# Mixer groups: the second gate block ahead of the turns of B and x, the rest one block later

## The reference

```
z, xbc, dt = split(u @ w_in)               # z: gate, xbc: x, B, C
xs, B, C = silu(causal_conv(xbc))
per chunk:  seg = exp(segment sums of dt*A)          # decay inside a chunk
            y   = (C B^T * seg) @ (x*dt) + exp(acs) * (C @ state)
            state = state * decay + B^T @ (x*dt * to_end)
y = rmsnorm((y + D*xs) * silu(z)) @ w_out
```

## Time and profile before

| | |
|---|---|
| median of 3 runs | 1906.42 us (1904.54 to 1907.23) |
| the profiled execution | 1900.23 us, span 1898.4 us |
| PE busy | 1832.8 us (97%) |
| weight loads of PE busy | 1742.0 us (92%) |
| DVE / ACT / POOL busy | 1140.4 / 825.7 / 249.8 us |
| mean granted clock of TensorE | 0.99 |
| the mixer's four groups | from 298 us to about 592 us of the span |

### The profile page before, as it was taken

How to read it: one execution, slowest core, us unless ns; L and a number is a source line. 1 busy time by engine, 2 the same in 40 slices (tenths; PEclk the granted TensorE clock), 3 DMA queues, 4 the chain that set the end, 5 groups by cost and what they waited for, 6 DMA issues and landing times.

```text
span 1898.4 us, 28238 instructions
## 1 busy us (share of the span) xinstructions
PE 1832.8 (97%) x10552; PEld 1742.0 (92%) x10552; DVE 1140.4 (60%) x1703; ACT 825.7 (43%) x1425; POOL 249.8 (13%) x298
## 2 busy tenths in 40 slices
PE   9999999999999999999999999988998999999997
PEld 8999998798887899999999999985777889999997
DVE  6554447878888655444765544455777746455444
ACT  5333325665464433333553333345665534333233
POOL 1000110422221000011400001222112130000110
PEclk9999999999999999999999999999999999999999
DMA  6444444456352544444344444441124533444441
GB/s 204 128 119 129 134 143 145 151 189 227 117 200 84 176 127 120 129 145 133 112 142 122 121 132 142 136 140 37 45 82 128 170 118 113 133 125 121 142 136 64
DMA packets 67652, 249.71 MB, mean 132 GB/s; under 512 B 8328, under 2 KB 9608, under 8 KB 66288
## 3 DMA queue, kind: packets, MB, share of 16 engines
q1 hardware_dynamic: 57584, 205.32, 35.9%
q0 software_dynamic: 9984, 43.24, 6.8%
HBM read 235.74 MB, written 12.12 MB: 131 GB/s over the span
## 4 chain that ended last, share of the span: by engine, by line
PE 83%; DVE 9%; ACT 4%; issue 2%; DMA 1%; POOL 0%; SPq 0%; DVEq 0%; ACTq 0%; POOLq 0%
PE pair L1805 23%; PE pair L1806 23%; PE pair L1807 23%; PE pair L2300 1%; PE pair L2218 1%; DVE wlo L1195 1%; PE pair L2219 1%; PE pair L2220 1%; DVE cy L1321 1%; PE pair L1812 1%; PE pair L1814 1%; PE pair L1813 1%; ACT seg L835 1%; PE pair L2002 1%; DVE S L1417 1%
## 5 line engine op out<-in xcount | busy, mean ns | idle before, releaser
L1805 PE MATMUL pair<-xh,whi 128*128 128x384 f32 x1928 | 652.9, 339 | 16.2 <-DVE xl L1205 13.4
L1806 PE MATMUL pair<-xl,whi 128*128 128x384 f32 x1928 | 647.1, 336 | 0.0
L1807 PE MATMUL pair<-xh,wlo 128*128 128x384 f32 x1928 | 646.9, 336 | 0.0
L1195 DVE TENSOR_TENSOR wlo<-raw,whi 128x1024 fp32r<-128x1024 f32 (+3 forms) x372 | 464.7, 1251 | 185.4 <-ACT whi L706 176.1
L706 ACT ACTIVATE whi<-raw 128x1024 fp32r<-128x1024 f32 (+2 forms) x369 | 378.7, 1029 | 290.8 <-PE pair L1807 276.7
L1805 PEld LDWEIGHTS pair<-xh,whi 128*128 128x128 f32 x1928 | 364.1, 189 | 26.3 <-issue 14.9
L1806 PEld LDWEIGHTS pair<-xl,whi 128*128 128x128 f32 x1928 | 364.3, 189 | 1.6 <-issue 1.0
L1807 PEld LDWEIGHTS pair<-xh,wlo 128*128 128x128 f32 x1928 | 364.1, 189 | 0.0
L1215 DVE TENSOR_TENSOR tg<-pair,rstd 128x384 f32<-128x384 f32 x88 | 49.0, 557 | 331.2 <-PE pair L1807 330.5
L1805 PE MATMUL pair<-ah,whi 128*128 128x384 f32 x704 | 237.0, 337 | 3.5 <-DVE tu L1216 3.3
L1807 PE MATMUL pair<-ah,wlo 128*128 128x384 f32 x704 | 236.6, 336 | 0.0
(11 more groups left out here) (394 smaller groups left out, 2285.1 us busy)
## 6 DMA issues: line engine op xcount, KB each, us to landing
raw<-in_stream SPq DMA_DIRECT2D x372, 512.0 KB, 3.6
S<-in_ssm POOLq DMA_DIRECT2D x4, 2048.0 KB, 9.2
out_ssm_s<-S POOLq DMA_DIRECT2D x4, 2048.0 KB, 8.1
seg<-acs_rows POOLq DMA_DIRECT2D x12, 512.0 KB, 6.1
cTb<-in_cacheT POOLq DMA_DIRECT2D x10, 512.0 KB, 4.0
kn<-rs_rows SPq DMA_DIRECT2D x16, 264.0 KB
lowC<-in_cache SPq DMA_DIRECT2D x8, 512.0 KB, 3.2
lowA<-in_cacheT POOLq DMA_DIRECT2D x6, 512.0 KB, 5.2
```

Of the source, the lines that this page charges most:

```text
L1195: V.tensor_tensor(wlo[:, r, 0:w], raw[:, r, 0:w], whi[:, r, 0:w].bitcast(F32), ALU.subtract).then_inc(lo_ready, 1)
L1805: M(out, whi[:, r, ws], mh_(k), start=first and k == k0, stop=False)
L1806: M(out, whi[:, r, ws], ml_(k), start=False, stop=False)
L1807: ins = M(out, wlo[:, r, ws], mh_(k), start=False, stop=last and k == k1 - 1)
```

## The change

PE multiplies block 7 ahead of the turns; block 8 stands where 7 was, 9 where 8 was. So nothing is left between `old_state`, `y_tile(g, 0)` and what follows. DVE takes blocks out in the same order; it makes all decays times the product (`decay_cb`) ahead of `evac(g, 9)`, then `y_old(g, 0)`, then `state_second`, and the `lo_split` that was part of `evac(g, 9)` comes last. In group 0 the third `decay_cb` stands between `y_old(g, 0)` and `state_second`. ACT, POOL and SP keep their streams.

```
@@ evac (VectorE) @@
                     V.tensor_tensor(zs[:, b - 6, :], src[:, 0:TOK], r, ALU.mult).then_inc(in_evac, 1)
-                if g or b:
+                if (g or b) and b < 9:
                     lo_split(n + 3)
@@ VectorE, the groups @@
                 in_proj(g, 6)
+                in_proj(g, 7)
                 b_rows(g)
                 g_mask(g)
                 if g == 0:
                     dve.wait_ge(da_ready, 1)
                 for t in range(TT):
                     x_rows(g, t)
-                in_proj(g, 7)
+                in_proj(g, 8)
                 state_first(g)
                 y_old(g, 1)
-                decay_cb(g, 0)
-                in_proj(g, 8)
+                for t in range(TT if g else 2):
+                    decay_cb(g, t)
+                evac(g, 9)
                 y_old(g, 0)
-                state_second(g)
-                decay_cb(g, 1)
-                if g:
-                    decay_cb(g, 2)
-                in_proj(g, 9)
                 if g == 0:
                     decay_cb(g, 2)
+                state_second(g)
+                lo_split(in_block(g, 9) + 3)
                 state_add(g, 0)
                 state_add(g, 1)
                 y_rows(g)
@@ TensorE, the groups @@
                 in_proj(g, 6)
+                in_proj(g, 7)
                 turns(g)
-                in_proj(g, 7)
+                in_proj(g, 8)
                 first_states(g)
-                in_proj(g, 8)
+                in_proj(g, 9)
                 old_state(g)
                 y_tile(g, 0)
-                in_proj(g, 9)
                 if last:
                     sample_states(g, 0)
                     y_tile(g, 1)
```

## The result

The changed kernel took 1918.8 us (median of 6, 1918.0 to 1920.1), the kernel before, run beside it, 1905.4 (6 runs, 1902.8 to 1907.2): a ratio of 1.0072, 95% interval 1.0059 to 1.0085. It is 13.4 us slower; the prediction had +10.4. The profiled execution took 1919.52 us, span 1917.7, so the two profiles stand 19.3 us apart. That is more than the 13.4 us between the medians, because the profiled execution of before was a short one, 5.2 us under its median (e9 looks at that). On the page PE's busy time rose from 1832.8 to 1844.8 us with the same matmuls: 12.0 of the 19.3 us are slower work, only 7.3 are waiting.

A forecast was written before the change was run, and what follows sets the result against it. PE, busy 97% of the span, was taken as the bound. Group 0 +0.7, groups 1 and 2 +1.1 each, group 3 +5.1 and clock +2.4 gave +10.4 us: 1910.6 on the profiled execution, 1916.8 by the median; range 1908.5 to 1920.

The forecast's parts named there:

- No wait at the turns: PE's waits at the turns of groups 0 and 3 both go, 1.83 and 2.06 us gained.
- first states of group 3: PE waits there for DVE's xw, a new wait of 2.6 us.
- the late split: Group 3: DVE stands about 5 us at block 7's lo_split, waiting for ACT's hi_split until 561.60.
- three decay_cb: In a row on DVE beside POOL's scaling: 5.6 us taken, bounds 3.4 to 5.6 us.
- groups 1 and 2: New PE waits of 0.4 and 0.7 us, together +1.1 us each; bounds 0 and about 1.6.
- idle time in group 0: PE idle about 3 us before the sample states; group 0 comes to +0.7 us (0.1 to 1.5).
- lower bound: Three decay_cb take 3.4 us if only alone-times count, without POOL waits.
- the clock: Half speed behind the long waits of groups 0 and 3: 1.2 us each, bounds 0 and 1.7, +2.4 in all.
- the first of group 3's waits: No clock cost counted behind the first states' wait, as PE has slack there.
- Rival C: Clock low twice as long after both waits, or after group 3's first wait too: +15, 1921.4 us; chance 0.08.
- The wait at the sample states of group 3: PE waits about 4.7 us for L1410; the group's shift is about +5.1 us.

The follow-up runs named there:

- e9: The kernel before, unchanged, profiled in one more execution: 1904.55 us, where its first profiled execution took 1900.2 us.
- e2: Changed kernel, in group 3 alone DVE's lo_split of block 7 + 3 goes behind the x_rows: 1910.2 us, 1.0033 to the kernel before.
- e6: Changed kernel, POOL scales only two of each head's 64 columns of the eight old states, all groups: 1913.2 us, 1.0045 to the kernel before.
- e8: New order in groups 1 and 2 alone, groups 0 and 3 as in the kernel before: 1907.5 us, 1.0020 to the kernel before.
- e11: Changed kernel with unused matmuls in its long new waits: four in group 0, five and seven in group 3; 1910.4 us, 1.0033 to before.
- e7: Kernel before with two unused matmuls ahead of the turns of groups 0 and 3: 1901.95 us, 0.9985 to the kernel before.
- e5: Changed kernel with four unused matmuls in each of its three long new waits (groups 0 and 3): 1914.6 us, 1.0052 to before.
- e4: Kernel before, in groups 0 and 3 the first half of block 7's products goes ahead of the turns: 1898.45 us, 0.9973 to before.
- e1: Changed kernel with unused matmuls, six ahead of group 3's first states, seven ahead of groups 0 and 3's first sample states: 1913.0 us, 1.0052 to before.
- e10: Half-block kernel (groups 0 and 3) with two unused matmuls ahead of group 0's decay sums: 1902.6 us, 0.9987 to the kernel before.
- e3: Changed kernel, in every group the decay_cb of tile 2 goes behind state_second: 1914.9 us, 1.0058 to the kernel before.

## Why the prediction was right, and where its sum was off

**Right, and by its steps.** Slower, 1916.8 forecast and 1918.8 measured; the step between the kernels was +10.4 forecast and +13.4 measured, and 1 us of the closeness comes from the base (1906.4 from three executions, 1905.4 from six). No wait at the turns; 3.09 us at the first states of group 3 for DVE's xw, where the sum had 2.6 (DVE idle 4.86 us for ACT's copy, "about 5" forecast), and e2 shows that it goes with the late split; three decay_cb in 5.84 us, 5.6 taken, and e6 shows POOL as the reason; +1.16 each in groups 1 and 2 against +1.1, and e8 gives the pair alone as +2.2; 3.35 us of idle time in group 0, "about 3". Without POOL's long instructions (e6, the eight scalings in 2.46 us) the three take 3.54 us, about the 3.4 us of the prediction's lower bound. That POOL gets in between the instructions was the author's estimate; the runs show only how much longer they take.

**The term that was mis-sized is the clock.** The prediction gave "1.2 us for each" of two waits, with 1.7 as its upper bound, +2.4 in all. By e11 the low clock behind the new waits was 8.4 us. Four things failed in that step. It took the length of the slow stretch from the one behind a later wait, 2.8 us; behind the sample states it was about 10 us, both times. It let the first of group 3's waits go free, where 1.75 us stood behind it. It said that some of the slow work would be waiting anyway: but in group 3 PE was busy 10.78 of 11 us at 0.53, and 4.7 of the 5.2 us lost to the clock came through. And it put the low clock that goes with the turns' waits at nothing, from one profile that had 1.00 behind both; e7 puts it at 3.4 us in the median. That is the one error which helped: the clock term is then +5.0 net and not +8.4, and part of the forecast's nearness is luck. Rival C had the longer stretches and the first wait, at +15 us with both, and was given 0.08; the measured +13.4 lies between it and the forecast, and nearer to C.

**A smaller one the other way.** The wait at the sample states of group 3 was put at 4.7 us and was 3.31. DVE's stretch from the three decay_cb to the end of L1410 came as forecast (580.08 to 589.08, 9.0 us). But PE, from the start of the first states to the end of y_tile(3, 0), took 11.7 us (574.18 to 585.91) where the sum had 9.8, since most of the first states ran at 0.50 (the mean from 574 to 578 is 0.72): the slow clock took part of the wait's place. The two terms aren't independent, which e5 shows from the other side: at full clock the same gap is 4.8 us.

The errors of the waits, -0.8 in group 3 and +0.4 in group 0, and +2.6 for the clock bring the +10.4 to +12.6, within the noise of +13.4. The part of this that is argued and not shown is that e7's 3.4 us are the clock behind the turns' waits: of the kernels with the old order in groups 0 and 3, only e8's trace has 0.50 there, the two of before don't.

## What to carry to other kernels

A block of matmuls between two steps is cover for whatever the other engines do there; before moving it, count what it covers behind as well as ahead, each engine's queue by itself. If the wait ahead is 2 us and the block 4, move half of it (e4).
Price a new wait on TensorE with the work behind it: here 7.3 us of new idle time in the profile came with 12.0 us of slower matmuls. And fill or shorten such a wait only up to the moment that the other engine sets, since filling past it is lost time: 2.2 us in e1, and in e10 the decay sums started 2.9 us later than in e4 (324.43 against 321.49).

## What the runs showed of the hardware beyond what was expected

- Stretches at 0.50 of about 10 us followed waits of 3.35 and 3.31 us in the changed kernel, where transposes and small matmuls came next, and also one of 2.36 us, with e10's filling of 384 columns and the decay sums next; behind group 3's first states, with a block next, 0.50 lasted some 3 us after a wait of 3.09 (changed kernel) and 7 us after one of 3.08 (e3). Waits of 1.17 (e6), 1.54 (e3) and 2.00 us (e5) were followed by 0.50, one of 1.62 us in e1 (group 0, y_tile 1) was not, and of e3's three equal waits of 1.5 us one was. So the length of a wait alone doesn't tell, and what does was not tested.
- The same 2 us wait at the turns of group 3, with the same work around it, was followed by 1.00 in two traces of before (2.06 us in both) and by 0.50 in that of e8 (2.12 us).
- DVE and POOL slow each other here: beside three decay_cb in a row (group 1, changed kernel) POOL's eight scalings took 12.67 us where they took 10.70 in the kernel before, and the three took 5.84 where they take 3.54 beside e6's short scalings. In group 3 of the changed kernel one decay_cb took 1.86 to 2.06 us and POOL's scalings beside them up to 2.02; in e6 one decay_cb took 1.21 to 1.27. No semaphore ties decay_cb to the scalings, so "on semaphores only" at the top leaves this out.
